# Turning the expert lists, asking for them six passes ahead, and twelve extra transposes before the last three passes of a decoder step

## The reference

```python
def moe(h, w_router, router_bias, w_gate_e, w_up_e, w_down_e, ...):
    scores = jax.nn.sigmoid(h @ w_router)
    sel = scores + router_bias
    ...                                   # best 4 of 8 expert groups
    _, eidx = lax.top_k(jnp.where(emask, sel, -jnp.inf), TOP_K)
    ...                                   # gates, normalised over the 8 chosen
    hg = jnp.einsum('td,edf->tef', h, w_gate_e)
    hu = jnp.einsum('td,edf->tef', h, w_up_e)
    act = jax.nn.silu(hg) * hu * gates[..., None]
    routed = jnp.einsum('tef,efd->td', act, w_down_e)
    ...
```

## Time and profile before

| | before |
|---|---|
| median of 3 runs | 1097.52 us |
| lowest and highest run | 1096.21 and 1099.22 us |
| the profiled execution, its time | 1099.3 us |
| the profiled execution, its span | 1097.5 us |
| TensorE busy | 934.3 us (85%) |
| VectorE busy | 404.1 us (37%) |
| ScalarE busy | 202.2 us (18%) |
| GpSimd busy | 242.0 us (22%) |
| mean granted clock of TensorE | 0.946 |
| moved by DMA | 289.66 MB |

### The profile page before, as it was taken

The page is one execution under the profiler, slowest core; times in us unless marked ns, Lnnn a source line. Parts: engine busy times, 40 slices in busy tenths (PEclk is TensorE's granted clock), DMA queues, the critical chain, the costliest instruction groups (busy, mean ns, idle before and its releaser), DMA issues.

```text
span 1097.5 us, 13692 instructions
## 1 busy us (share of the span) xinstructions
PE 934.3 (85%) x4773; PEld 440.3 (40%) x4773; DVE 404.1 (37%) x975; ACT 202.2 (18%) x415; POOL 242.0 (22%) x301
## 2 busy tenths in 40 slices
PE   4979987997988889799899897899797979999784
PEld 3564555465534544333333332333232324333231
DVE  5957447857873652123111111111111111111116
ACT  6050031141213131111111110111110111111103
POOL 1910029002300166102111211112111210222012
PEclk9989998998999899899899998999898999999988
DMA  9720120231226118899999999999999999999945
GB/s 325 304 77 5 74 78 0 77 90 70 47 79 231 46 55 346 359 377 385 394 381 384 385 389 392 376 381 374 370 394 382 372 374 376 359 339 388 381 147 195
DMA packets 66421, 289.66 MB, mean 264 GB/s; under 512 B 17291, under 2 KB 18539, under 8 KB 41392
## 3 DMA queue, kind: packets, MB, share of 16 engines
q1 hardware_dynamic: 45376, 250.21, 57.7%
q0 software_dynamic: 13232, 35.04, 12.2%
q10 hardware_dynamic: 7744, 3.53, 1.2%
HBM read 257.14 MB, written 41.18 MB: 272 GB/s over the span
## 4 chain that ended last, share of the span: by engine, by line
PE 47%; issue 29%; DVE 13%; ACT 5%; DMA 4%; ACTq 1%; SPq 0%; POOL 0%; DVEq 0%; POOLq 0%
PE bank L998 24%; PE bank L1944 21%; DVE arena L1592 3%; DVE arena L698 2%; PE bank L1036 2%; DMA prm<-expert_lists 1%; DVE arena L800 1%; ACT arena L1265 1%; DMA sum_rows<-arena,xs 1%; ACT arena L1252 1%; DVE bb L720 1%; DMA qkv_samples<-arena 1%; DVE arena L1923 1%; DMA arena<-in_x_prompt 1%; DVE arena L1905 1%
## 5 line engine op out<-in xcount | busy, mean ns | idle before, releaser
L998 PE MATMUL bank<-arena 128*32 128x512 f32 (+6 forms) x2930 | 539.7, 601 | 82.2 <-issue 52.9
L998 PEld LDWEIGHTS bank<-arena 128*32 128x32 f32 (+3 forms) x2930 | 198.3, 132 | 391.1 <-issue 376.4
L1944 PE MATMUL bank<-arena 128*128 128x512 f32 (+9 forms) x1208 | 309.2, 444 | 32.7 <-ACT arena L1549 8.5
L1944 PEld LDWEIGHTS bank<-arena 128*128 128x128 f32 (+4 forms) x1208 | 173.0, 191 | 162.3 <-issue 128.8
L465 POOL DMA_INDIRECT arena<-h_rows,xs x42 | 43.6, 1039 | 466.7 <-DVE bb L720 455.3
L698 DVE SCALAR_TENSOR_TENSOR arena<-arena,xs,bank 128x256 f32<-128x256 f32 x42 | 27.7, 660 | 312.1 <-issue 271.5
L695 DVE COPY arena<-bank 128x512 f32<-128x512 f32 x41 | 28.4, 692 | 179.1 <-PE bank L998 174.6
L554 ACT ACTIVATE arena<-bank 128x256 f32<-128x256 f32 x42 | 16.1, 383 | 328.7 <-PE bank L998 284.2
L474 POOL DMA_INDIRECT sum_rows<-arena,xs x41 | 64.6, 1576 | 53.4 <-DVE arena L695 30.6
L1592 DVE TENSOR_TENSOR arena<-arena 64x512 f32<-64x512 f32 (+8 forms) x79 | 68.3, 865 | 6.5 <-DMA arena<-o_samples 3.8
L484 POOL DMA_INDIRECT expert_lists<-arena,ncim x40 | 39.8, 994 | 91.4 <-issue 87.7
(11 more groups left out here) (231 smaller groups left out, 529.1 us busy)
## 6 DMA issues: line engine op xcount, KB each, us to landing
arena<-in_w_gate_e SPq DMA_DIRECT2D x64, 1024.0 KB, 18.4
arena<-in_w_up_e SPq DMA_DIRECT2D x64, 1024.0 KB, 34.5
arena<-in_w_down_e SPq DMA_DIRECT2D x64, 1024.0 KB, 33.8
arena<-in_w_in SPq DMA_DIRECT2D x5, 2048.0 KB, 9.0
expert_lists<-arena SPq DMA_DIRECT2D x1, 8482.5 KB, 28.9
arena<-in_x_prompt SPq DMA_DIRECT2D x8, 512.0 KB, 5.9
arena<-in_w_out SPq DMA_DIRECT2D x2, 2048.0 KB, 8.3
arena<-sum_rows SPq DMA_DIRECT2D x8, 512.0 KB, 7.9
```

The costliest lines, as they stand in the source:

```text
L998: return nc.tensor.matmul(o, l, r, start=start, stop=stop, skip_group_check=True)
L1944: return nc.tensor.matmul(o, l, r, start=start, stop=stop, skip_group_check=True, **kw)
```

## The change

Lists. Neighbouring tuples of the same expert are joined to whole segments (`segments`), so three thirds become one segment of 96. From pass 4 on, each segment is turned by k places, k from 0 to 15 by a running count (`turned`): place c0 + k holds the first entry, and the last k entries go to places c0 to c0 + k - 1. So a segment is loaded by two DMAs of width - k and k rows, or by one where k is 0. In all there are 137 list DMAs where there were 110. The register with the expert's number is read once for each segment. The first DMAs of the lists have widths such as 83, 89, 93, 59 and 117 where they had 32, 64 and 128. The constant `c_unit` is turned with them.

Ahead. The list of pass u+6 is asked for at the end of pass u, where it was pass u+4. The lists of passes 4 and 5 are asked for right before the loop of passes.

Transposes. In the last three passes TensorE does twelve transposes of the unit matrix into bank 7 in front of the first projections; no instruction reads them.

```diff
+AHEAD = 6
...
+def segments(u):
+
+    parts = []
+    for r, c0, width, first in UNITS[u]:
+        if parts and parts[-1][0] == r and parts[-1][3] + parts[-1][2] == first:
+            parts[-1] = (r, parts[-1][1], parts[-1][2] + width, parts[-1][3])
+        else:
+            parts.append((r, c0, width, first))
+    return parts
+
+
+SEGMENTS_BEFORE = [sum(len(segments(w)) for w in range(u)) for u in range(NU)]
+
+
+def turned(u):
+
+    parts = []
+    for n, (r, c0, width, first) in enumerate(segments(u)):
+        k = 5 * (SEGMENTS_BEFORE[u] + n) % 16 if u >= LISTS else 0
+        parts.append((r, c0 + k, width - k, first))
+        if k:
+            parts.append((r, c0, k, first + width - k))
+    return parts
+
+
 def lists_landed(u):
 
-    return 16 * sum(len(UNITS[w]) for w in range(u % LISTS, u + 1, LISTS))
+    return 16 * sum(len(turned(w)) for w in range(u % LISTS, u + 1, LISTS))
...
-            for r, c0, width, first in UNITS[u]:
-                e = act.value_load(order_i[0:1, r:r + 1], min_val=0, max_val=NE - 1)
+            e, known = None, None
+            for r, c0, width, first in turned(u):
+                if r != known:
+                    e, known = act.value_load(order_i[0:1, r:r + 1], min_val=0, max_val=NE - 1), r
                 act.dma_start(lists[u % META][c0:c0 + width, :],
...
-            if u + LISTS < NU:
-                act_list(act, u + LISTS)
+            if u + AHEAD < NU:
+                act_list(act, u + AHEAD)
...
             act_rows(act, 0)
+            for u in range(LISTS, AHEAD):
+                act_list(act, u)
             for u in range(NU):
                 act_unit(act, u)
...
+        def stay_busy(n):
+
+            for _ in range(n):
+                nc.tensor.transpose(bank[7][:, 0:P], ident[:], ident[:])
+
...
             for u in range(NU):
+                if u >= NU - 3:
+                    stay_busy(12)
                 pe_up(pe, u)
...
     for u, tiles in enumerate(UNITS):
+        for r_, c0, width, first in turned(u):
+            unit[c0:c0 + width, u] = first + np.arange(width)
         for r_, c0, width, first in tiles:
-            unit[c0:c0 + width, u] = first + np.arange(width)
             unit[c0:c0 + width, 64 + u] = TT * ACCS[u][r_] - FAR
```

## The result

The change makes the kernel slower: median 1126.66 us against 1096.87 us for the kernel before on the same chip, ratio 1.0245 (95% interval 1.0173 to 1.0318). Measured a second time it took 1117.94 us, ratio 1.0198 (1.0166 to 1.0231). The forecast was 1089.5 us and the range ended at 1110: wrong in sign.

The account below looks back on a forecast made before the run. The passes were taken to go at the pace of weight DMAs, the engines fuller with gather and scatter rows being slowest. Span 1097.5 - 7 (Part 1) - 0 - 0 - 1 (Part 4) = 1089.5 us; range 1082 to 1110.

Parts of the forecast that it names:

- 11 us of work left undone in the tail: DMA windows at the end: how much earlier the mean engine is through, the upper bound on evening out there.
- Part 2: List issues on ScalarE's queue: whole lists, fewer register reads, more DMAs; up to 2.2 us more a pass, hidden, cost nothing.
- Part 3: Lists asked for six passes ahead: lead from 14.5 to 43.5 us, cover for late lists, value 0.
- Rival A: Odd-width list pieces fall on one DMA engine, lists land late, VectorE waits: 1107 us, chance 0.22.
- Part 1: Turned lists even out gather and scatter rows over the DMA engines, at about 0.50 us a row: 7 us less.
- sixteenths: Sharing of a gather's 128 places where an engine serves every sixteenth place: fullest engine 292 rows to 265, 13 us less.
- eight neighbours: Sharing of a gather's places where an engine serves eight neighbouring places: fullest engine 336 rows before and after, nothing won.
- two groups of four: Sharing where an engine serves two groups of four neighbouring places 32 apart: fullest engine 330 rows to 313, 8 us less.
- Part 4: Twelve transposes before the last three passes' first projections: hidden in waits, likely hold TensorE's clock; 1 us gained, bounds 1.7 gained, 1.6 lost.

Follow-up runs that it names:

- cut pieces: The change with each odd-width list piece cut into a multiple of 16 rows and a remainder: 1097.45 us, ratio 0.9991 to the kernel before; without transposes 1094.94 us.
- by 16s: The change turned by multiples of 16 places: 1083.10 us; without transposes 1081.99; without them and lists four ahead 1080.87, ratio 0.9841 to the kernel before.
- by 8s: The change turned by multiples of 8 places, six ahead, without the transposes: 1075.71 us, ratio 0.9798 to the kernel before.
- by 4s: The change turned by multiples of 4 places, uncut, six ahead, without the transposes: 1075.68 us, ratio 0.9793 to the kernel before.
- odd pieces without a turn: The change with every list entry in its unturned place, but lists still asked for in the change's odd widths: 1147.55 us, ratio 1.0460 to the kernel before.

## Why the prediction was wrong, point by point

**What bounds the kernel: right.** The pace was set by engines with more rows than others; evening them out won up to 21 us (below). The 11 us of work left undone in the tail, given as a bound from above for the tail, were too small a measure of the whole; a likely reason is that what the fuller engines cost in earlier passes no longer shows at the end.

**Part 2, the step that failed.** It put the issues at 0.83 to 0.96 us each, from pieces of 32, 64 and 128 rows, and hid them under the first projections, "cost nothing". The durations came from widths that all divide by 16, and the change's don't. The issue right behind an odd piece took up to 15.25 us, far beyond the 6.28 and 6.44 us of idle time that were to cover it. What is behind it on the queue, the Silu, had been named, and so had the price without cover, but only for 2.2 us a pass. The cost of the odd widths is the change against the same placement with cut pieces and the same transposes: 1126.66 or 1117.94 against 1097.45, 20 to 29 us.

**Part 3: right on both counts.** The lead alone is worth at most some 2 us (0.9984 with whole lists; with 16s, four ahead took no longer than six), and it is cover: with four ahead the change takes 1144.48 us. But "it adds no wait of ScalarE" overlooked that an issue itself can wait.

**Rival A: the right cause on the wrong path.** Odd widths, one engine, lists that queue up: yes. But it let the lists land late and VectorE wait, and decided by the summed landing against 43.5 us of lead. The issue behind an odd piece was held before any list was late, and ScalarE stood still with the Silu behind it. With four ahead its wait appears as well. Its 1107 us was under the 1112 to 1127 measured, and its chance of 0.22 too low: the widths were in the diff, and the value taken for Part 2 had no row of such a width.

**Part 1: the mechanism right, the size wrong.** The fullest engine's rows by each sharing, counted from the lists' lengths, against the time won over the kernel without a turn (ratios of the kernels without transposes, times 1098.3 us):

| turn | sixteenths | eight neighbours | two groups of four | won, us |
|---|---|---|---|---|
| none | 292 | 336 | 330 | 0 |
| 0 to 15 (the change's, cut) | 265 | 336 | 313 | 1.8 |
| by 16s | 292 | 288 | 289 | 13.6 |
| by 8s | 274 | 293 | 275 | 20.4 |
| by 4s | 270 | 286 | 273 | 21.0 |

Only the fourth column is in the order of the times. At the 0.50 us a row of the prediction (Part 1), 313, 289, 275 and 273 rows fit a start of 317, 316, 316 and 315 rows, not of 330. So the price and the sharing fit, and the mis-sized term is the count before: the pace goes as if the fullest engine had some 316 rows. Why not 330 stays open; no view names an engine. By the Trainium skill (DMA: Bandwidth & Descriptors, "The descriptor swizzle") a transfer to 128 partitions is shared as in the fourth column; by that rule, the order of the times agrees.

**Part 4: half right.** In every kernel that has the transposes in the last passes the last projections took 7.09 us, behind waits of up to 2.23 us. Without a turn, and without them, the last projections took 8.78 us behind a wait of 1.97; with them 7.09 behind 2.21. These are the two kernels, without and with, from the last projections on:

```profile
1055.85 8.78 PE L1028 MATMUL bank<-arena 128*64 128x512 f32 x32 [1.97 <-issue]
...
1066.85 3.65 PE L1028 MATMUL bank<-arena 128*64 128x512 f32 x16 [0.62 <-issue]
1071.67 7.88 PE L1028 MATMUL bank<-arena 128*128 128x512 f32 x24 [1.16 <-ACT arena L576]
```

```profile
1056.17 7.09 PE L1028 MATMUL bank<-arena 128*64 128x512 f32 x32 [2.21 <-issue]
...
1065.49 5.35 PE L1028 MATMUL bank<-arena 128*64 128x512 f32 x16 [0.62 <-issue]
1073.25 7.85 PE L1028 MATMUL bank<-arena 128*128 128x512 f32 x24 [2.41 <-issue]
```

That the transposes held the clock is likely from this pair, and from the kernel before without and with them, but not shown. Over waits of 3.3 to 4.5 us one or two passes earlier they did not hold it (8.45 to 9.94 us). And without any, projections of 7.09 us stand behind waits of 1.49 us in the last pass (turned and cut) and of 2.18 and 3.93 us in earlier passes (without a turn).

The 1.7 us are won there and lost in the next step: the down projections take 5.35 us instead of 3.65. This step is not tied to the transposes: in the kernels turned by 8s and by 4s, without them, it also took 5.35 us behind projections of 7.09, and on the kernel before with them 3.65. Windows over them (columns as in the earlier trace rows), without and with, have the clock at 1.00 and 0.62:

```profile
1066.90:1070.50 3.60, 3.60 (x16) 1.00 1.02 331
```

```profile
1065.50:1067.50 2.00, 2.00 (x6) 0.62 1.04 414
```

The late last matmuls come on top (2.41 for 1.16). Forecast 1 won; measured 3.9 lost on the kernel before, and on three others 0.4 to 2.5 lost (ratios 1.0003 for 0.9984, 0.9991 for 0.9968, 0.9864 for 0.9860). The Trainium skill (TensorE: Matmul & The Clock Gate, "PE-mode transpose") says that transposes do not count as busy in the same way for the clock; the two pairs lean against it and do not settle it.

**Open:** why the change's runs spread from 1112 to 1127 us. Both of its profiles are from the lower end and look alike (waits for the gated product 62.4 and 61.5 us from 465 us on); none of an execution near 1127 was seen.

## What to carry to other kernels

When a change gives a DMA new sizes, price its issue by rows of such sizes or treat it as unknown: a width that 16 does not divide may go over one engine, and the packet count on the page tells it. The issue behind such a DMA can stand still, and everything behind it on that engine's queue with it, so ask what stands there before calling a load early and cheap. Placement and request can be separated: turning by 8 or 4 places kept the evening-out that the change was after, without odd pieces.

## What the runs showed of the hardware

- A list DMA's issue on ScalarE's queue took 0.32 us in the median of the kernel before, and up to 15.25, 18.05 and 18.10 us right behind a piece of 83 or 89 rows (the change, odd pieces without a turn, four ahead); the issue of that piece itself took 0.47 us. With 540 list rows on the fullest engines, counted as above, the longest issue was 0.60 us; with 1,807 it was 15.25.
- 36 more transposes on TensorE, at either of the two places tried, moved the wait ahead of its last matmuls from 1.16 us to between 2.41 and 4.40 us; the matmuls then began 1.58 to 1.66 us after a packet of instructions had landed.
- TensorE's granted clock fell from 1.00 to a mean of 0.62 over 2 us behind a wait of only 1.17 us and two transposes, in the down projections of the last pass without a turn and with the added transposes, where TensorE had waited 2.21 us shortly before. Turned by 8s it fell to a mean of 0.70 at the same place, where the wait shortly before was 0.41 us and there were no added transposes.
